# Sums of squares added up on VectorE ahead of the post norms, and ten runs of small matmuls joined to their neighbours

## The reference

```python
def rms_norm(x, g):
    xf = x.astype(jnp.float32)
    y = xf * lax.rsqrt(jnp.mean(xf * xf, axis=-1, keepdims=True) + EPS)
    return (y * g.astype(jnp.float32)).astype(x.dtype)
...
    for i in range(DEPTH):
        h = rms_norm(x, g[0])
        h = mlstm_mixer(...) if i % N_MIXERS == 0 else short_conv_mixer(...)
        x = x + rms_norm(h, g[1])
        h = sqrelu_mlp(rms_norm(x, g[2]), w_mlp_up[i], w_mlp_down[i])
        x = x + rms_norm(h, g[3])
```

## Time and profile before

| | |
|---|---|
| median of 3 timed executions | 971.26 us (963.71 to 972.72) |
| profiled execution | 966.34 us |
| its span, first to last instruction | 964.5 us |
| mean granted TensorE clock | 0.996 |
| TensorE busy | 946.8 us, 98% |
| VectorE, ScalarE, POOL busy | 640.9, 536.2, 99.0 us |
| DMA | 172.19 MB, 179 GB/s |

### The profile page before, as it was taken

One profiled execution on the slowest core, in us unless ns is written; L12 is line 12 of the kernel. 1 busy time (PEld: TensorE's weight loads), 2 busy tenths in 40 slices (PEclk: granted clock), 3 DMA queues, 4 the chain that ended last, 5 costly groups with the idle time before them and its releaser, 6 DMA issues.

```text
span 964.5 us, 20171 instructions
## 1 busy us (share of the span) xinstructions
PE 946.8 (98%) x8078; PEld 939.0 (97%) x8078; DVE 640.9 (66%) x878; ACT 536.2 (56%) x757; POOL 99.0 (10%) x96
## 2 busy tenths in 40 slices
PE   9999999999999999999999999999999999999997
PEld 8999999999999999999999999999999999999997
DVE  5767577665444886678665444793766679999742
ACT  6566647654444555556565444465554567666542
POOL 0111100000010000108100000005030020000001
PEclk9999999999999999999999999999999999999999
DMA  9533545555554354544555553644352445555531
GB/s 338 211 131 127 210 145 208 185 193 199 192 200 175 144 204 176 178 172 176 202 190 201 192 189 124 245 178 172 115 192 88 175 164 187 204 188 205 196 123 44
DMA packets 26421, 172.19 MB, mean 179 GB/s; under 512 B 3444, under 2 KB 4084, under 8 KB 6136
## 3 DMA queue, kind: packets, MB, share of 16 engines
q1 hardware_dynamic: 26072, 171.04, 49.5%
q10 hardware_dynamic: 288, 0.27, 0.1%
HBM read 170.24 MB, written 1.05 MB: 178 GB/s over the span
## 4 chain that ended last, share of the span: by engine, by line
PE 82%; DVE 4%; ACT 1%; issue 1%; POOL 0%; POOLq 0%; DVEq 0%; ACTq 0%
PE po L433 24%; PE po L434 24%; PE po L435 24%; DVE wL L1364 1%; PE po L460 1%; PE po L461 1%; PE po L462 1%; PE third L433 1%; PE third L434 1%; PE third L435 1%; PE pn L523 1%; PE pc L796 1%; ACT wH L880 1%; PE pn L533 0%; PE third L774 0%
## 5 line engine op out<-in xcount | busy, mean ns | idle before, releaser
L1364 DVE TENSOR_TENSOR wL<-raw,wH 128x1024 fp32r<-128x1024 f32 x316 | 385.5, 1242 | 164.3 <-ACT wH L880 164.0
L880 ACT ACTIVATE wH<-raw 128x1024 fp32r<-128x1024 f32 x316 | 331.5, 1057 | 233.6 <-PE po L435 210.1
L433 PE MATMUL po<-xnH,wH 128*128 128x256 f32 x1296 | 364.5, 281 | 8.5 <-DVE wL L1364 5.9
L434 PE MATMUL po<-xnL,wH 128*128 128x256 f32 x1296 | 359.7, 278 | 0.0
L435 PE MATMUL po<-xnH,wL 128*128 128x256 f32 x1296 | 359.7, 278 | 0.0
L433 PEld LDWEIGHTS po<-xnH,wH 128*128 128x128 f32 x1296 | 243.5, 188 | 10.0 <-issue 6.6
L435 PEld LDWEIGHTS po<-xnH,wL 128*128 128x128 f32 x1296 | 244.4, 189 | 0.0
L434 PEld LDWEIGHTS po<-xnL,wH 128*128 128x128 f32 x1296 | 243.7, 188 | 0.2
L435 PE MATMUL po<-hH,wL 128*128 128x256 f32 x688 | 189.9, 276 | 0.0
L433 PE MATMUL po<-hH,wH 128*128 128x256 f32 x688 | 189.9, 276 | 0.0
L434 PE MATMUL po<-hL,wH 128*128 128x256 f32 x688 | 189.9, 276 | 0.0
(11 more groups left out here) (309 smaller groups left out, 1146.6 us busy)
## 6 DMA issues: line engine op xcount, KB each, us to landing
raw<-in_weights SPq DMA_DIRECT2D x157, 1024.0 KB, 4.8
raw<-in_weights SPq DMA_DIRECT2D x4, 256.0 KB, 5.1
raw<-in_weights SPq DMA_DIRECT2D x2, 512.0 KB, 7.1
mem<-in_memT SPq DMA_DIRECT2D x1, 1024.0 KB, 12.5
out<-y SPq DMA_DIRECT2D x4, 256.0 KB, 2.6
x<-in_xT SPq DMA_DIRECT2D x3, 256.0 KB, 5.3
decayt<-in_decay SPq DMA_DIRECT2D x1, 512.0 KB, 3.6
x<-in_xT ACTq DMA_DIRECT2D x1, 256.0 KB, 3.7
```

Source lines behind the costliest of these rows:

```text
L433: pe.matmul(psum[:, n, 0:T], wH[w][:, wc], aH[:, ac, :], start=start, stop=False)
L434: pe.matmul(psum[:, n, 0:T], wH[w][:, wc], aL[:, ac, :], start=False, stop=False)
L880: act.activation(wH[b % HL][:, hs], raw[b % RAW][:, hs], ACT.Copy).then_inc(s_hi, 1)
L1364: dve.tensor_tensor(wL[b % HL][:, hs], raw[b % RAW][:, hs], wH[b % HL][:, hs].bitcast(f32), ALU.subtract)\
```

## The change

- **Post norms.** VectorE adds the two chunks of the fourth group of squares, and adds the result to POOL's (`last_square`), so `norm_sums` has one product for each half of the tokens instead of three. It stands behind step 2 of the first filler instead of step 1, and `norm_spread` behind step 5 of the first filler in all four boundaries.
- **Boundaries on VectorE.** With one filler (n = 4) the split of the second slab's first half moves behind the first pair of x, the other half behind `add(2)`; one more half moves from ahead of `feed_pair(2)`.
- **Joined runs.** `gates` in two runs of 8 products; in o `norm_sums(1)` with `numerator(0)`, `norm_spread(1)` with `numerator(1)`, `turn_head(0)` with `numerator(2)`, `turn_head(1)` with `numerator(3)`; in attention `xa_scores(2)` with `xa_turn(0)`, `xa_values(0)` with `xa_turn(1)`, `xa_scores(3)` with `xa_values(1)`, `xa_values(3)` with `spacer`.
- **Halves of splits and drains** change places in o (slab 13), in rq (slabs 4 and 5 from its start) and ahead of out2.
- **First loads.** SP issues the first gains ahead of all else, no longer ScalarE.

```diff
-            return sum(k == "preV" for k in NORMS[:norm])
+            return sum(k in ("preV", "post") for k in NORMS[:norm])
...
+            sp.dma_start(par[:, 0:C], params[:, 0:C]).then_inc(s_gain0, 16)
             for q in range(4):
...
-                pe.wait_ge(s_sq, 4 * n + 4)
                 for t in range(TT):
-                    tc = slice(t * P, t * P + P)
-                    squared = [sq[0][:, 0, tc]]
-                    if NORMS[n] in ("post", "last"):
-                        squared += [sq[3][:, 0, tc], sq[3][:, 1, tc]]
-                    for k, chunk in enumerate(squared):
-                        mm = pe.matmul(pn[:, t:t + 1], chunk, ones[:, 0:1], start=k == 0, stop=k == len(squared) - 1)
+                    mm = pe.matmul(pn[:, t:t + 1], sq[0][:, 0, t * P:t * P + P], ones[:, 0:1], start=True, stop=True)
...
-                gates(1, range(4))
-
-            phase_slab("qk", 1, xnH, xnL, between={6: lambda: gates(0, range(4)), 7: lambda: gates(0, range(4, 8))})
-            phase_slab("qk", 2, xnH, xnL, between={0: sums_and_gates, 1: lambda: gates(1, range(4, 8)), 3: lambda: norm_spread(0)})
+                gates(1, range(8))
+
+            phase_slab("qk", 1, xnH, xnL, between={7: lambda: gates(0, range(8))})
+            phase_slab("qk", 2, xnH, xnL, between={0: sums_and_gates, 3: lambda: norm_spread(0)})
...
-            phase_slab("o", 0, xnH, xnL, between={0: lambda: numerator(0), 1: lambda: norm_sums(1), 5: lambda: norm_spread(1),
-                                                  6: lambda: numerator(1)})
-            phase_slab("o", 1, xnH, xnL, between={1: lambda: turn_head(0), 2: lambda: numerator(2), 6: lambda: turn_head(1),
-                                                  7: lambda: numerator(3)})
+            phase_slab("o", 0, xnH, xnL, between={1: lambda: (norm_sums(1), numerator(0)), 6: lambda: (norm_spread(1), numerator(1))})
+            phase_slab("o", 1, xnH, xnL, between={2: lambda: (turn_head(0), numerator(2)), 7: lambda: (turn_head(1), numerator(3))})
...
-                spread = lambda: norm_spread(n_norm)
-                fill(names[0], {1: lambda: norm_sums(n_norm)} | ({} if names[1:] else {3: spread}))
+                fill(names[0], norm(n_norm, 2, 5))
                 for n in names[1:]:
-                    fill(n, {0: spread})
+                    fill(n)
...
-            phase_slab("wq", 3, xnH, xnL, between={1: lambda: xa_turn(0), 3: lambda: xa_scores(2), 4: lambda: xa_values(0),
-                                                   6: lambda: xa_turn(1)})
-            fill(7, {1: lambda: xa_scores(3), 2: lambda: xa_values(1), 4: lambda: xa_turn(2), 6: lambda: xa_values(2)})
+            phase_slab("wq", 3, xnH, xnL, between={2: lambda: (xa_scores(2), xa_turn(0)), 5: lambda: (xa_values(0), xa_turn(1))})
+            fill(7, {1: lambda: (xa_scores(3), xa_values(1)), 4: lambda: xa_turn(2), 6: lambda: xa_values(2)})
...
-                           between={0: lambda: xa_turn(3), 2: lambda: xa_values(3), 3: spacer} if i == 0 else {})
+                           between={0: lambda: xa_turn(3), 2: lambda: (xa_values(3), spacer())} if i == 0 else {})
...
-            act.dma_start(par[:, 0:C], params[:, 0:C]).then_inc(s_gain0, 16)
...
+            mix_hi(mixf[:, :, :], 3, (s_mixf, 4))
             split(v0 + 9, halves=(1,))
-            mix_hi(mixf[:, :, :], 3, (s_mixf, 4))
...
-            split(u0 + 7)
+            split(u0 + 7, halves=(0,))
             mix_hi(ret_y[0][:, :, :], 2, (s_ry, 1))
             silu_g(1)
             mix_hi(ret_y[1][:, :, :], 3, (s_ry, 2))
+            split(u0 + 7, halves=(1,))
...
+            def last_square(n):
+
+                dve.wait_ge(s_sq, 4 * n + 4)
+                link(dve.tensor_tensor(sq[3][:, 0, :], sq[3][:, 0, :], sq[3][:, 1, :], ALU.add))
+                dve.wait_ge(s_sqa, squares_added(n + 1))
+                dve.tensor_tensor(sq[0][:, 0, :], sq[0][:, 0, :], sq[3][:, 0, :], ALU.add).then_inc(s_sqv, 1)
...
+            keep_o(3)
             mix_lo(mixf[:, :, :], 2, 2)
-            keep_o(3)
-            split(13, halves=(0,))
             gated(3)
             mix_lo(mixf[:, :, :], 3, 3)
-            split(13, halves=(1,))
+            split(13)
...
                 split(first, halves=(0,))
+                last_square(n)
                 mean_square(n)
                 split(first, halves=(1,))
-                split(first + 1, halves=(0,))
+                if two:
+                    split(first + 1, halves=(0,))
...
+                if i >= 2:
+                    split(r0 + i + 2, halves=(0,))
...
                 if i >= 2:
-                    split(r0 + i + 2)
+                    split(r0 + i + 2, halves=(1,))
...
+            keep("rg", 1, rsg[:, 2:4, :])
             ret_scaled(1)
-            keep("rg", 1, rsg[:, 2:4, :])
```

32 lines of the change are left out of this document (21 added, 11 removed).

## The result

| | before | after |
|---|---|---|
| median of the timed executions | 971.26 us (963.71 to 972.72) | 956.70 us (955.00 to 962.39) |
| profiled execution | 966.34 us | 960.92 us |
| its span | 964.5 us | 959.1 us |

The ratio is 0.9886, 95% interval 0.9847 to 0.9924: 1.1% faster. It isn't the ratio of the medians (0.985): the five executions of each kernel scatter by 7 to 9 us, and their means are 968.97 and 958.25 (0.989). The prediction was 958.5 us, from 950 to 967.

A forecast was written before the change was run, and what follows sets the result against it. TensorE, busy 98% of the span, was taken to bound the kernel by instructions times pace, plus waits. Terms 7.95 + 0.3 + 0.7 + 0.6 + 0.2 + 0.2 = 9.95 us off 968.5 gave 958.5 us, range 950 to 967.

The forecast's parts named there:

- The three boundaries: Boundaries with two fillers (n = 2, 6, 8): 0.90 from removed sums plus 1.75 of wait gone, 2.65 us each, 7.95 in all.
- the upper bound: At each boundary with two fillers: 2.7 us if VectorE's whole chain moves earlier, against 0.90 if it doesn't.
- Rival 2: VectorE's chain takes the gain: added adds or power hold the spread up, boundaries give only 0.90; 964.1 us, chance 0.20.
- The boundary at `cin`: Boundary with one filler (n = 4): removed sums mostly turn into new waits; 0.3 us gained, bounds 0 and 2.4.
- `rq`: In `rq`, the low half TensorE waited for starts ahead of a drain and a product: 0.7 us gained.
- `out0`: Into `out0`, a half-slab split and a wait for ScalarE move behind, TensorE's 0.5 wait goes: 0.6 us with refilling.
- `out2`: Into `out2`, the drain of `rg` moves up: 0.2 us gained.
- The first loads: At the start, SP issues the first gains, ScalarE starts 0.4 earlier, other loads later: 0.2 us gained, bounds +0.4 and -0.5.
- Joined runs: Ten runs of small matmuls joined to a neighbour: 0.1125 us per instruction alone or joined, so 0 saved at equal pace.
- The clock at the gates: Drop to the lower clock behind the gates, priced at 1.5 us, left as it is; bounds -1.5 and +1.5.
- The level: Starting time of the whole kernel before: 968.5 us, the mean of four executions.
- Rival 3: Long stretches fall to the slow pace: 971 us with two slow, 977 with three; chance 0.10.

The follow-up runs named there:

- spread_early: Before with sums behind step 2 and spread behind step 5 of the first filler, 12 sum instructions kept, no added adds; 960.58 us, ratio 0.9936.
- norms_only: Before with the new post norms and boundaries alone; 956.94 us, ratio 0.9895.
- cin_old_order: After with VectorE's order of before at the boundary with one filler; 958.80 us, one execution.
- loads_only: Before with the moved first loads alone; 972.50 us, one execution.
- best: After with the first loads moved back and the ten joined runs apart again; median 954.72 us, ratio 0.9813.
- joined_only: Before with the ten joined runs of small matmuls alone; median 974.13 us, ratio 1.0086.
- loads_back: After with the first gains issued by ScalarE's queue again; 955.04 us, one execution.
- after_again: After, unchanged, run again; 954.44 us, one execution.
- no_spacer: After without the small product of unused result ahead of the last feed-forward; 959.66 us, ratio 0.9882.
- two_spacers: After with two small products of unused result, instead of one, ahead of the last feed-forward; 961.73 us, ratio 0.9912.
- after_timed: After, unchanged, timed once more in a later set; 962.27 us, ratio 0.9901.
- best_cin: best with the sums of norm 5 one step later in the `cin` pair and its spread two; 952.32 us, ratio 0.9825.

## Why the prediction was right, point by point

- **The three boundaries**: predicted 2.65 each, measured 2.61, 2.66 and 2.58. Every step came where it was put: sums 120.40 (120.29), spread 122.97 (122.86), first scaling 123.9 (123.94), TensorE on at 131.3 (131.28), with f4 itself 0.11 us earlier than assumed. The reason for taking the upper bound held, that one row (1.58 us idle, ended by the spread) set the start of all behind it; spread_early shows it by itself. The new start is the one that the prediction named too, the split for which ScalarE waits on the filler's fourth step. Rival 2 needed late adds or a late power: the adds had 0.3 us to spare, and the spread stands with no idle time ahead.
- **The boundary at `cin`**: predicted a gain of 0.3, measured 0 (norms_only 19.8) to a loss of 0.25 (after, with a drop of the clock). The waits that it named came, 0.78 for x, 0.94 for a half slab, and 1.11 for squares in norms_only. The weak step is "the chain ... holds that split in addition, so it ends only some 0.3 us earlier": the chain did hold it and ended 0.1 earlier, but I read the place of the split as given and didn't ask what the old place would cost now. With the spread at the same time and the sums' wait gone, the old place lay in idle time, and cin_old_order has the 0.84 us that the new order gave away (19.80 to 18.96).
- **`rq`**: 0.7, measured 0.9 (20.29 to 19.04 us for the same matmuls, less 0.33 of pace). **`out0`**: 0.6, measured 0.8 (22.66 to 21.86). **`out2`**: 0.2, measured 0.35. All a little small, 0.5 in sum.
- **The first loads**: predicted +0.2, measured a loss of 0.36 (loads_only) to 0.54 (after), and 0.64 in the mean of seven traces against seven. The sign was wrong. The failed step is "the gain of 0.4 mostly ends there": it looked at one slab. The feed came 1.5 us sooner, not 0.4, and TensorE caught up with weights that land later, in two slabs. The loss lies about at the bound of -0.5.
- **Joined runs**: predicted 0, measured 0 to 0.15 lost. 16 instructions in one run cost 1.79 us.
- **The clock at the gates**: predicted unchanged, and it shows 0.79 in before and in after. The prediction's price of the drop, 1.5 us, is what the traces show: from the first gates to the log sums it is 17.05 us in before and 15.50 in best and loads_only. The Trainium skill ("TensorE: Matmul & The Clock Gate", Part 1) has activity release the clock, and light work speaks against it. The drops here do follow the gates, but the same gates run with and without one. That before and after both had one was luck.
- **Not foreseen**: 0.36 us gained in `fup`, where the spread of norm 11 waited for POOL's power in the kernels with the old norms and in none with the new. Then a wait of 0.60 us for xnL at the start of `wq`, which isn't the change's. It stands in the eleven traces whose `out2` ran at the fast pace, loads_only with before's program among them. It is missing in the three (before, joined_only, loads_back) whose `out2` ran at the slow pace, loads_back with the change's program among them. There `out2` takes 0.7 us more and `wq` 0.7 less. So the pace term counts some 0.8 us as saved by pace in after that was no time saved, and the change is worth as much more.
- **Sum**: 9.95 predicted, 8.4 and 8.6 measured without pace, so about 9.3 with the 0.8 of `wq` put right. The miss is `cin` (0.3 to 0.55), the loads (0.7) and the joins (0.15), less some 0.8 by which `rq`, `out0`, `out2` and `fup` came out larger. Parts of a few tenths on both sides cancel here.
- **The level**: 968.5 as a start was the mean of four executions; the pace term of single executions lay between 5.5 and 15.6 us, so 5 us either way were never the program's. The median of after fell 1.8 below the forecast, which is luck as much as it is the sum: the medians are 14.6 us apart, the means 10.7, and the traces without pace 9.3. Rival 3 came true for one long stretch (the last feed-forward of the profiled execution, 6.5 us), where two were needed to decide.

## What to carry to other kernels

Find the row at which a chain begins (idle time ended by the thing you would move), and price a moved step by what starts behind it: here the place gave 1.7 us and the removed instructions 0.9. When something comes earlier, look again at what else stood around it; a split that had been moved out of the way would have been free in its old place. Joining small work into fewer runs gave nothing where each instruction keeps its own price, and before a gain of a few us is believed, compare stages in traces, since whole times move by as much between executions.

## What the runs showed of the hardware

- **Two paces at one granted clock.** 113.1 and 117.6 ns for the same matmul form, both at PEclk 1.00 and without idle time; a stretch of 150 us or more keeps one of them, and the same program takes the last feed-forward in 173.5 or 180 us. The slow pace came there in 4 of the 7 profiled executions with the gains issued first on SP, and in none of the 7 without. after_again, no_spacer and two_spacers have the moved loads and the fast pace, so the loads don't settle it; whether they make it likelier stays open.
- **The same kernel between sets of runs.** Before had 966.03 in one set and 971.90 and 971.95 in the next two, each set on another chip. Within the last set, on one chip, it took 964.01 once and 969.23 to 975.32 otherwise. Only ratios inside a set are compared here.
- **The clock's drop at the gates** gave 0.79 over 22 to 30 us in eight traces (before, norms_only, joined_only, spread_early, after, after_again, after_timed, two_spacers), 0.65 in no_spacer, 0.57 in loads_back and 1.00 in best, best_cin, loads_only and cin_old_order; 59 instructions were done in after, 44 in loads_back and 71 in best. From the first gates to the log sums a short drop costs 1.6 to 1.8 us and the long one of loads_back and no_spacer 3.1 (with joined gates: 14.79 without, 16.37 in after, 17.94 in loads_back). The six traces of the change's own start show all three cases. Both long drops have joined gates, and three of the four without a drop have them apart; whether the joins matter, fourteen traces don't tell.
- **A second drop** stands in after in the `cin` pair, behind waits of 0.78 and 0.94 us. The window there, with busy time (xinstructions) of TensorE, its weight loads, VectorE, ScalarE and POOL, then PEclk, DMA share and GB/s:

```profile
315.00:319.00 4.00, 3.95 (x21) 3.98 (x22) 3.96 (x7) 2.11 (x5) 0.00 (x0) 0.57 0.00 0
```

It is the 0.25 us by which after is behind norms_only (19.8 to 20.05), whose clock is 1.00 in the same window. More time was lost than that, but it lay where norms_only waits 1.11 us for squares, a wait that after hasn't. after_again, after_timed, best and no_spacer have this drop too, and in the last three the stage takes 17.76, as good as the 17.71 to 17.73 of norms_only, loads_back and two_spacers, which have the wait for squares instead: there the drop costs next to nothing.
